# Output projections of two mixer layers as seven half-size float32 products with block sums on VectorE

## What is computed

```python
def layer(x):
    hcur = rms_norm(x, norm1_g) * (1 + sc1) + sh1
    proj = hcur @ w_in
    # layer one: dilated attention (channels 0 to 511), gated mlp (512 to 1023)
    # layer two: convolution (channels 0 to 511), stick-breaking attention (512 to 1023)
    mixed = concatenate([o_a, o_b], -1)      # (256, 1024)
    x = x + g1 * (mixed @ w_out)             # w_out is (1024, 1024): the part that changes
    hcur = rms_norm(x, norm2_g) * (1 + sc2) + sh2
    x = x + g2 * hierarchical_moe(hcur)      # sixteen experts, top two of one group
```

## Time and profile before

| what | value |
|---|---|
| median of 3 runs | 1172.2 us (1169.63 to 1173.45) |
| the profiled execution | 1169.14 us, span 1167.5 us |
| TensorE busy | 1110.4 us, 95% of the span |
| VectorE busy | 435.8 us, 37% |
| DMA | 353.83 MB, mean 303 GB/s |

### The profile page before, as it was taken

One profiled execution on the slowest core, in us unless ns is written; L12 is line 12 of the kernel. 1 busy time (PEld: TensorE's weight loads), 2 busy tenths in 40 slices (PEclk: granted clock), 3 DMA queues, 4 the chain that ended last, 5 costly groups with the idle time before them and its releaser, 6 DMA issues.

```text
span 1167.5 us, 17066 instructions
## 1 busy us (share of the span) xinstructions
PE 1110.4 (95%) x6882; PEld 646.8 (55%) x6883; DVE 435.8 (37%) x1082; ACT 273.0 (23%) x579; POOL 91.9 (8%) x156
## 2 busy tenths in 40 slices
PE   3999999999999999989999999998999999999998
PEld 0766534444444378564444444443886877757883
DVE  0275244122111089962611111113541353342554
ACT  2214332111111031062311111113101555542101
POOL 0300030000000000140000000000011334200000
PEclk8899999999999999999999999999999999999999
DMA  9999799999999987994999999999595454444000
GB/s 363 354 326 395 221 403 362 421 428 429 429 427 429 412 322 292 297 310 152 379 375 429 427 429 429 428 428 391 189 290 182 157 173 141 130 158 135 24 19 36
DMA packets 69381, 353.83 MB, mean 303 GB/s; under 512 B 5541, under 2 KB 7757, under 8 KB 49869
## 3 DMA queue, kind: packets, MB, share of 16 engines
q1 hardware_dynamic: 61656, 340.68, 75.8%
q0 software_dynamic: 6000, 9.17, 2.9%
q10 hardware_dynamic: 1668, 3.21, 0.8%
HBM read 350.84 MB, written 1.15 MB: 301 GB/s over the span
## 4 chain that ended last, share of the span: by engine, by line
PE 77%; DMA 15%; DVE 4%; ACT 2%; issue 1%; ACTq 0%; SPq 0%; DVEq 0%
PE bank L504 29%; PE bank L877 20%; DMA ring<-in_moe_w_up 13%; PE bank L542 7%; PE bank L833 3%; PE bank L898 2%; DMA arena<-in_ev_w_s 2%; PE bank L1243 2%; DVE arena L1767 2%; PE bank L557 1%; PE bank L1153 1%; PE bank L528 1%; PE bank L516 1%; PE bank L718 1%; PE bank L733 1%
## 5 line engine op out<-in xcount | busy, mean ns | idle before, releaser
L504 PE MATMUL bank<-arena,ring 128*128 128x256 f32 x1536 | 342.3, 383 | 1.9 <-ACT arena L1315 1.7
L877 PE MATMUL bank<-ring,arena 128*32 128x512 f32 x3072 | 335.4, 593 | 6.6 <-DMA ring<-in_moe_w_up 3.3
L504 PEld LDWEIGHTS bank<-arena,ring 128*128 128x128 f32 x1536 | 292.1, 192 | 48.0 <-issue 8.7
L877 PEld LDWEIGHTS bank<-ring,arena 128*32 128x32 f32 x3072 | 103.1, 110 | 225.5 <-issue 223.6
L542 PE MATMUL bank<-ring,arena 128*128 128x512 f32 x224 | 98.3, 594 | 0.0
L2287 DVE TENSOR_TENSOR arena<-arena,bank 128x512 f32<-128x512 f32 x16 | 11.0, 688 | 191.5 <-PE bank L877 191.5
L542 PEld LDWEIGHTS bank<-ring,arena 128*128 128x128 f32 x224 | 42.0, 190 | 50.3 <-issue 50.0
L833 PEld LDWEIGHTS bank<-arena 128*128 128x128 f32 x512 | 58.5, 192 | 12.0 <-issue 11.7
L833 PE MATMUL bank<-arena 128*128 128x128 f32 x512 | 61.2, 278 | 0.0
L898 PE MATMUL bank<-arena 128*128 128x512 f32 x128 | 57.7, 594 | 0.0
L1767 DVE SCALAR_TENSOR_TENSOR arena<-arena,cv 128x256 f32<-128x256 f32 x144 | 57.6, 484 | 0.1
(11 more groups left out here) (339 smaller groups left out, 958.2 us busy)
## 6 DMA issues: line engine op xcount, KB each, us to landing
ring<-in_moe_w_gate SPq DMA_DIRECT2D x32, 2048.0 KB, 14.8
ring<-in_moe_w_up SPq DMA_DIRECT2D x32, 2048.0 KB, 17.2
ring<-in_moe_w_down SPq DMA_DIRECT2D x32, 2048.0 KB, 13.3
ring<-in_w_ada SPq DMA_DIRECT2D x24, 2048.0 KB, 21.6
ring<-in_w_in SPq DMA_DIRECT2D x16, 2048.0 KB, 11.8
ring<-in_w_c SPq DMA_DIRECT2D x6, 2048.0 KB, 33.1
ring<-in_ev_w_in SPq DMA_DIRECT2D x5, 2048.0 KB, 14.3
ring<-in_od_w_in SPq DMA_DIRECT2D x5, 2048.0 KB, 15.5
```

Of the source, the lines that this page charges most:

```text
L504: mm = pe.matmul(ps[k0][:, t * S:(t + 1) * S], w[:, k, c:c + P], rhs[:, k, :], start=(k == 0), stop=(k == KT - 1))
L877: mm = pe.matmul(bank[col:col + CHUNK, :], lhs[:, k, col:col + CHUNK], ring[:, (s0 + e) % RING, cut], start=start, stop=stop, tile_positio ...
```

## The change

Each projection is computed as a product of 2 x 2 blocks by 2 x 2 blocks with seven block products in place of eight. A block product is four matmuls of 128x128 by 128x512 (half of the channels of 128 tokens against half of the rows and half of the columns of the matrix). VectorE forms four block sums of the weights (`mix_columns`, `w12`, `mix_three`, `mix_all`, each 128x2048 elements a partition row) and four of the tokens (each 128x512), in buffers that are free at that time. Both weight units are needed for the first block sums: `column_differences` waits for both loads. In layer one it stands ahead of `gating` in VectorE's order, and two more weight sums stand between `gating` and `group_cols(2)`. In layer two it stands ahead of the scaling of the convolution, and the two other weight sums stand in `routed_norm`. `routed_norm` reads three partial products early, so that three banks serve twice. The two parts of the modulation group and the turns of the two tiles now alternate, and ScalarE takes the first turned tile after it has scaled its half of the second. In layer two ScalarE copies the last heads ahead of a table load. Semaphore counts in the third block are shifted to fit, nothing else there changes.

```diff
+        mix_columns, mix_three, mix_all = at(8, 4, HW), at(0, 4, HW), at(36, 4, HW)
+        m_difference, m_second, m_three, m_all = (at(28 + 2 * n, 4, P) for n in range(4))
+        mix_squares = at(48, TT, D)
+        tile_products = pr[:, 0, :], pr[:, 1, :], prT
+        MIXES = {1: ("evo0", "evo1"), 3: ("odo0", "odo1")}
+        def mix_blocks(r):
+            return [slot_of[name][:, rows, :] for name in MIXES[r] for rows in (slice(4, 8), slice(0, 4))]
...
-            def heads_out(b, k):
-                if b == 0 and k == 0:
-                    pe.wait_ge(sem("o_taken"), 8)
-                elif b == 0 and k == 4:
+            def gating_there(k):
+                if k == 4:
                     pe.wait_ge(sem("gmlp_ready"), 3)
-            def first_tile(r):
-                def arrived(b, k):
-                    if b == 1 and k == 5:
-                        turn_tile(r, 0)
-                return arrived
-            by_token("evo0", oT, arrived=heads_out)
-            by_token("evo1", oT, arrived=first_tile(1))
-            group_main(3, (0, 1))
-            turn_tile(1, 1)
+            def stick_there(k):
+                pe.wait_ge(sem("o_taken"), 8 + 2 * (k - 3))
+            def mixed_products(r, near_there, far_sem, far_count, group):
+                first, second = MIXES[r]
+                round_ = r // 2
+                w1, w2 = weights(), weights()
+                near, far = slice(4, 8), slice(0, 4)
+                def product(bank, tokens, w, start, done):
+                    for k in range(4):
+                        mm = pe.matmul(ps[bank][:, :], tokens[:, k, :], w[:, k, :], start=(start and k == 0), stop=(k == 3),
+                                       skip_group_check=True)
+                    mm.then_inc(done, 1)
+                b0 = bank_of(first, 0)
+                for k in range(4, 8):
+                    near_there(k)
+                    mm = pe.matmul(ps[b0][:, :], oT[:, k, P:S], w1[:, k, :], start=(k == 4), stop=(k == 7),
+                                   skip_group_check=True)
+                mm.then_inc(sem("product_full"), 1)
+                b1 = bank_of(first, 1)
+                pe.wait_ge(sem("token_sums"), 4 * round_ + 1)
+                pe.wait_ge(sem("o_weights"), 4 * round_ + 2)
+                product(b1, m_difference, w2[:, near, :], True, sem("product_full"))
+                pe.wait_ge(sem(far_sem), far_count)
+                pe.wait_ge(sem("product_added"), 3 * round_ + 1)
+                product(b0, oT[:, far, P:S], w1[:, far, :], False, bank_full[b0])
+                b2 = bank_of(second, 0)
+                pe.wait_ge(sem("token_sums"), 4 * round_ + 3)
+                pe.wait_ge(sem("o_weights"), 4 * round_ + 3)
+                product(b2, m_three, mix_three, True, sem("product_full"))
+                pe.wait_ge(sem("o_weights"), 4 * round_ + 4)
+                pe.wait_ge(sem("product_added"), 3 * round_ + 2)
+                product(b1, oT[:, far, 0:P], mix_all, False, unit_done)
+                pe.wait_ge(sem("product_added"), 3 * round_ + 3)
+                product(b2, m_second, mix_columns, False, bank_full[b2])
+                b3 = bank_of(second, 1)
+                pe.wait_ge(sem("token_sums"), 4 * round_ + 4)
+                product(b3, m_all, w2[:, far, :], True, unit_done)
+                group_main(group, (0,))
+                turn_tile(r, 0)
+                group_main(group, (1,))
+                turn_tile(r, 1)
+            mixed_products(1, gating_there, "o_taken", 8, 3)
...
+            mixed_products(3, stick_there, "conv_ready", 2, 6)
...
-                for n, (t, h) in enumerate(((0, 0), (1, 0), (0, 1))):
+                for n, (t, h) in enumerate(((1, 0), (0, 0), (0, 1))):
                     act.wait_ge(sem("x_half"), 4 * no + n + 1)
-                    square_half(t, h, xn)
+                    square_half(t, h, mix_squares)
                 act.wait_ge(sem("x_sum"), 4 * no + 3)
                 tile_root(0, no, sq(0, 1))
-                tile_out(r, 0)
                 act.wait_ge(sem("x_half"), 4 * no + 4)
-                square_half(1, 1, xn)
+                square_half(1, 1, mix_squares)
                 act.wait_ge(sem("x_sum"), 4 * no + 4)
                 tile_root(1, no, sq(1, 1))
                 second_tile(r)
-                tile_out(r, 1)
+                for t in range(TT):
+                    tile_out(r, t)
...
+                stick_out(p)
                 if p == 3:
                     act.preload_act_table(ACT.Silu)
-                stick_out(p)
...
-            def add_mixed(name, half, b, tmp):
-                n, cols_ = dense[name], slice(half * 512, half * 512 + 512)
-                src, free = full_at(dve, name, b)
-                dve.tensor_tensor(tmp[b], src[:, :], gate_bc[:, cols_], ALU.mult).then_inc(free, 1)
-                dve.wait_ge(bank_free[2 * (n % 2) + b], n // 2 + 1)
-                dve.tensor_tensor(x[:, b, cols_], x[:, b, cols_], tmp[b], ALU.add).then_inc(sem("x_half"), 1)
+            def weight_difference(out_, a_, b_, after):
+                dve.wait_ge(sem("o_weights"), after)
+                dve.tensor_tensor(out_, a_, b_, ALU.subtract).then_inc(sem("o_weights"), 1)
+            def token_sum(out_, a_, b_, op, after):
+                dve.wait_ge(sem("token_sums"), after)
+                dve.tensor_tensor(out_, a_, b_, op).then_inc(sem("token_sums"), 1)
+            def column_differences(r):
+                for name in MIXES[r]:
+                    n = unit_of[name]
+                    dve.wait_ge(loaded[n % RING], 16 * (n // RING + 1))
+                w11, w21, w12, w22 = mix_blocks(r)
+                weight_difference(mix_columns, w12, w11, 4 * (r // 2))
+                weight_difference(w12, w22, w12, 4 * (r // 2) + 1)
+            def three_blocks(r):
+                w11, w21, w12, w22 = mix_blocks(r)
+                weight_difference(mix_three, w22, mix_columns, 4 * (r // 2) + 2)
+            def all_blocks(r):
+                w11, w21, w12, w22 = mix_blocks(r)
+                weight_difference(mix_all, w21, mix_three, 4 * (r // 2) + 3)
+            near, far = slice(4, 8), slice(0, 4)
+            def near_difference(r):
+                token_sum(m_difference, oT[:, near, P:S], oT[:, near, 0:P], ALU.subtract, 4 * (r // 2))
+            def second_and_three(r):
+                token_sum(m_second, oT[:, near, 0:P], oT[:, far, 0:P], ALU.add, 4 * (r // 2) + 1)
+                token_sum(m_three, m_second, oT[:, near, P:S], ALU.subtract, 4 * (r // 2) + 2)
+            def all_tokens(r):
+                token_sum(m_all, oT[:, far, P:S], m_three, ALU.subtract, 4 * (r // 2) + 3)
...
+            read_wait(dve, unit_of["ev3"])
+            column_differences(1)
             gating()
+            three_blocks(1)
+            all_blocks(1)
             group_cols(2)
             gain(1)
-            def routed_norm(r, names):
-                no = r - 1
-                tmp = (pr[:, 0, :], pr[:, 1, :])
+            def routed_norm(r, beside_products):
+                no, round_ = r - 1, r // 2
+                first, second = MIXES[r]
+                t0, t1, t2 = tile_products
+                def times_gate_row(tmp, bank, half, read, count):
+                    dve.tensor_tensor(tmp, bank[:, :], gate_bc[:, half * 512:half * 512 + 512], ALU.mult).then_inc(read, 1)
+                    dve.wait_ge(read, count)
+                def bank_read(name, b):
+                    n = dense[name]
+                    src, free = full_at(dve, name, b)
+                    return src, free, n // 2 + 1
+                def add(t, h, tmp, last=False):
+                    step.wait()
+                    ins = dve.tensor_tensor(half_of(x, t, h), half_of(x, t, h), tmp, ALU.add)
+                    if last:
+                        ins.then_inc(sem("x_half"), 1)
+                    else:
+                        step(ins)
+                n = dense[first]
+                dve.wait_ge(sem("product_full"), 3 * round_ + 1)
+                bank = ps[2 * (n % 2)]
+                step(dve.tensor_tensor(t0, bank[:, :], gate_bc[:, 512:1024], ALU.mult))
+                times_gate_row(t1, bank, 0, sem("product_added"), 3 * round_ + 1)
+                beside_products()
+                dve.wait_ge(sem("product_full"), 3 * round_ + 2)
+                times_gate_row(t2, ps[2 * (n % 2) + 1], 1, sem("product_added"), 3 * round_ + 2)
+                add(0, 1, t0)
+                add(1, 1, t0)
+                add(0, 0, t1)
+                add(0, 1, t2)
+                src, free, count = bank_read(first, 0)
+                times_gate_row(t0, src, 0, free, count)
+                add(1, 0, t0, True)
                 step(dve.tensor_tensor(sel, ident[:, 0:20], ident[:, 32:52], ALU.add))
                 for g in (2, 3):
                     step.wait()
...
                     if g == 2:
                         step(ins)
```

(37 more changed lines are left out.)

61 lines of the change are left out of this document (20 added, 41 removed).

## The result

The changed kernel takes 1174.35 us in the median of 15 runs (1170.19 to 1176.88), the kernel before 1170.34 us in as many (1167.16 to 1173.45). The ratio is 1.0037, 95% interval 1.0024 to 1.0050: slower by 4.0 us, where 6.7 us were forecast. The profiled execution has a span of 1171.4 us, 3.9 us more than before. TensorE is busy 1100.6 us (94%) in place of 1110.4, VectorE 470.8 us (40%) in place of 435.8; the DMA volume is the same 353.83 MB. TensorE does 9.8 us less and the kernel ends 3.9 us later, so 13.7 us of new waiting are to be found.

A forecast was written before the change was run, and what follows sets the result against it. TensorE was taken as the bound in both layers' products. Layer one 9.0 us later, layer two 2.3 us sooner: 6.7 us on the median 1172.2 us gives 1178.9 us, range 1171.5 to 1184.5 us.

The forecast's parts named there:

- Removed work: TensorE, each projection: 64 matmul instructions become 56, 8 x 0.431 = 3.45 us less in each layer.
- The landing of evo1: Layer one's second weight unit, issued at 119.8 us, lands 14.5 us later, at 134.3 us, and the weight differences wait for it.
- The start: Layer one: differences until 139.0 us, gating until 142.0 us, TensorE's first product there instead of 132.39 us, 9.7 us lost.
- The second product: Layer one: waits for the token difference until 147.75 us, 2.3 us more lost; this hides the lower clock, taken as 0.
- The end of layer one: Second turn at 173.3 us, routing sums at about 175.2 us in place of 166.31 us; 9.0 us later by terms.
- The term of 0.4 us for taking two tiles at the end: Layer one's end: ScalarE takes both tiles after its own scaling, adding 0.4 us before the routing sums.
- GpSimd: Layer one: its write begins 13.7 us later; read-back covered by 5.6 us, `rpb_sent` by 1.3 us, so no cost.
- The experts: After layer one: TensorE and the load stream shift nearly alike, the whole 9.0 us kept, 1.5 us of give in the range.
- Layer two: Projection to routing sums: 0.7 us lost at product six plus 0.45 us for two tiles minus 3.45 us, 2.3 us sooner.
- with the lower clock until 527.5 us, as before: Layer two's first product: starts at 523.6 us at the lower clock, as before, and ends at 528.8 us.
- the weights land sooner: Rival, layer one: evo1 there at 127.9 us, second product 6.4 us before the forecast; 1172.5 us, no change; chance 0.16.
- The wait is not paid: Rival, layer one: evo1 there by about 120.5 us, differences done before gating; -5.4 us, 1166.8 us; chance 0.06.

The follow-up runs named there:

- difference first: The changed kernel with layer one's near token difference moved right behind the gating, ahead of the last two weight sums; ratio 1.0043 to the kernel before.
- layer one only: The kernel before with the change made in layer one alone, layer two keeping the old functions; ratio 1.0077 to the kernel before.
- satisfied waits: The changed kernel with long-satisfied TensorE semaphore waits put behind each layer's last projection turn, 22 and 24 of them; ratio 1.0054 to the kernel before.
- the first experiment: The changed kernel with layer one's weight sums made from the left weight unit alone, so VectorE need not wait for evo1; 1251.36 us, total not usable.
- sums behind: The changed kernel with layer one's VectorE order changed: gating and token difference first, weight sums after; ratio 0.9981 to the kernel before.
- far first: The changed kernel with layer one's weight sums behind the gating and its far-block product second; ratio 0.9954 with added satisfied waits, 0.9957 without.
- wait-only run: The kernel before with only a VectorE wait for layer one's right weight unit added ahead of the gating, no weight sums; ratio 1.0040.
- changed again: The changed kernel run once more, unchanged; ratio 1.0034 to the kernel before.
- layer two only again: Second run of the kernel before with the change made in layer two alone, layer one as before; ratio 0.9969 to the kernel before.

## Why the prediction was right, by its steps

The sign, the size within a factor of two, and the place were right. **Removed work**: 8 instructions of 0.431 us in each layer; layer two at equal clock gives 3.1 us after a loss of 0.4, as the sum said. **The landing of evo1**: 14.4 us against 14.5, at 134.1 us; in the four other profiles with this order it took 15.3 to 15.6 us, and the differences start at 135.3 to 135.5 us. **The start**: differences from 134.12 us, gating from 138.65, first product at 141.81 for 142.0 us. **The second product** at 147.50 us for 147.75, but with two causes, not one. I wrote that the wait for the token difference hides the lower clock and took 0 for the clock; the clock was low for 10.2 us, not one stretch of 3.4 us, and the first product took 5.86 us. My 2.3 us stood for both, and the run with the difference first shows that the clock alone would have cost them. The level was right, the length was not.

**The end of layer one.** 174.55 us against about 175.2. The term of 0.4 us for taking two tiles at the end was the wrong one: from the end of product seven to the sums it takes 6.3 us, where the old form took 5.5 us plus 0.9 us for the turn inside the products. The net is about 0, in layer two as well. In the five profiles with this order in layer one (changed twice, layer one only, difference first, satisfied waits) the sums start at 174.55 to 176.28 us, 8.2 to 10.0 us later than before, with 9.0 forecast.

**GpSimd** was covered, and by more than I had: both its wait and its read-back were shorter than before (the DMA engines were nearly idle at that time, see the last section). **The experts** kept the whole shift, 8.2 us at 192.14, 370.12 and 399.48 us, so the give of 1.5 us was not used.

**Layer two** is the term that was mis-sized: -2.3 forecast, -4.8 in the profile, -3.1 at equal clock. Product six waited 0.4 us (10.86 for 10.46 us over the three products), not 0.7; the two tiles cost nothing, not 0.45. The rest, 1.7 us, came from "with the lower clock until 527.5 us, as before": whether that stretch is there changes from one execution to the next. Among the profiles of this study it is there in some with the old layer two and away in others, and the same holds for the new one (32.7 us against 31.0 us in the table).

The forecast of +6.7 us was 2.7 us too high by the medians and 2.8 us by the profiles. In these, 0.8 us is layer one, 0.8 us layer two at equal clock and 1.7 us the clock stretch there; 1.1 us were won back before it, 0.8 us between its sums and the gather, and 0.8 us after the experts' start; 3.2 us at the gather, nearly all of it the stall, work against that. That the total came so near is in part luck: in this execution 6.0 us of terms that I had too high or didn't have met 3.2 us the other way. The sum had no term for the stall, and the stretches of lower clock stood only in the range. Of the rivals, "the weights land sooner" had the wrong premise: evo1 took 14.4 to 15.7 us in all fourteen profiles. The prediction's reason against it, a slow ramp in an otherwise quiet queue, is only a part: from the issue to the landing the windows of the changed kernel add up to about 3.8 MB, nearly twice the 2 MB of evo1, so the modulation loads issued behind it from 122.2 us on moved alongside. "The wait is not paid" is what the first experiment built: worth 10.7 us at the sums, and still not the 12 us of free sums. Its price in the prediction took no account of evo0, which in that run landed only at 123.5 us.

## What to carry to other kernels

When work on a late input is put into an engine's queue, look at what is queued behind it: by the start of the routing sums the change cost 8.2 us with the weight sums ahead of the gating, 1.5 us with them behind it, and nothing with the far product second as well. Order the consumer's products so that those that need no new input come first, and break a long gap into short ones; the gaps of 1.54 and 0.98 us also kept the clock, where 3.51 us was followed by half clock. Price the saving at the bound engine against its new waits in each place by itself: here one of two identical edits gained 3.1 us and the other at best broke even in the orders that were tried.

## What was not expected of the hardware

- A wait of 3.5 us (sums behind) was followed by 3.4 us at half clock, about 1.7 us of work; waits of 1.54 and 0.98 us (far first), and of 1.46 us in the wait-only run, were not. In between it isn't settled: 2.06 us of waiting ahead of layer two's products were followed by half clock in the kernel before, 2.05 us in the changed kernel were not. In a standstill of 9.7 us the clock fell to half 3.9 us after TensorE had stopped and stayed there for 10.2 us; around one of 10.6 us it was at half for 13.7 us, more than half of each while TensorE stood still anyway.
- TensorE can stand for up to 3.06 us at the first expert of layer two, by the times of the fetches most likely for its own instructions. The same kernel showed 3.06 us in one execution and none in the next.
- A load of 2 MB took 14.4 us again in a queue that had run dry. No bytes moved from 119.8 to 123.2 us, 182 GB/s until 126.2 us, and the window in which it ended moved 423 GB/s, shared with the loads behind it. The Trainium skill, DMA: Bandwidth & Descriptors, "Bandwidth", has 425 GB/s for large transfers; the trace agrees for a queue that is running, and not for the first microseconds after it ran dry.
- The same load of evo0 landed 12.6 to 15.8 us after its issue in ten of the fourteen profiles, and 23.0 to 24.0 us after it in four (before, changed again, layer two only again, no wait for evo1). In the last of them the DMA engines moved nothing from 116.8 to 121.8 us, and the landing came at 123.5 us all the same. Why stays open.
- GpSimd's read-back of 4 KB landed in 1.9 us in place of 6.8 us. Its new time is one at which the DMA engines were nearly idle: a share of 0.06 and 4 GB/s from 158.5 to 160.5 us, where before it was 1.00 and 362 GB/s from 147 to 154 us. No run varies that alone.
